# Block one's up projection: a 512-column matmul for the convolved half of pairs 2 to 21, and where the bank rotation starts

## What is computed

```python
h = modulate(rms_norm(x, norm_ffn[l]), sh2, sc2)
x = x + gt2[:, None, :] * conv_gated_ffn(h, ffn_w_up[l], ffn_conv_w[l], ffn_conv_b[l], ffn_w_down[l])
```

## Time and profile before

| | |
|---|---|
| time, median of 3 runs (lowest, highest) | 2118.98 us (2118.73, 2119.17) |
| the profiled execution's own time | 2120.44 us |
| its span | 2118.5 us |
| granted TensorE clock, mean | 1.00 |
| busy: TensorE, weight loads, VectorE, ScalarE, GpSimd | 99%, 90%, 77%, 58%, 1% |

### The profile page before, as it was taken

How to read it: one execution, slowest core, us unless ns; L and a number is a source line. 1 busy time by engine, 2 the same in 40 slices (tenths; PEclk the granted TensorE clock), 3 DMA queues, 4 the chain that set the end, 5 groups by cost and what they waited for, 6 DMA issues and landing times.

```text
span 2118.5 us, 39184 instructions
## 1 busy us (share of the span) xinstructions
PE 2095.2 (99%) x16348; PEld 1902.0 (90%) x16348; DVE 1639.5 (77%) x2519; ACT 1235.6 (58%) x2010; POOL 13.1 (1%) x20
## 2 busy tenths in 40 slices
PE   8999999999999999999999999999999999999999
PEld 7898999999998899998888989888898888998888
DVE  7899789888887788877887656787688765778876
ACT  4754755555755656555655448566475644766554
POOL 0000000000000000000000000000000000000000
PEclk9999999999999999999999999999999999999999
DMA  9566567768644467655555654555555567455553
GB/s 371 198 210 216 175 214 256 243 226 288 224 158 171 163 209 239 204 181 188 188 190 189 230 159 154 203 190 189 189 180 189 189 196 223 140 170 209 189 189 130
DMA packets 122099, 424.57 MB, mean 200 GB/s; under 512 B 13457, under 2 KB 22033, under 8 KB 121154
## 3 DMA queue, kind: packets, MB, share of 16 engines
q1 hardware_dynamic: 121922, 422.06, 59.0%
HBM read 417.68 MB, written 4.33 MB: 199 GB/s over the span
## 4 chain that ended last, share of the span: by engine, by line
PE 90%; ACT 4%; DVE 4%; DMA 1%; issue 1%; POOL 0%; SPq 0%; ACTq 0%; DVEq 0%
PE bank L207 89%; ACT arena L258 2%; DVE arena L213 2%; DMA raw<-W 1%; ACT hi L258 1%; DVE lo L213 1%; PE bank L210 1%; ACT L258 1%; DVE arena L221 0%; DVE ada L230 0%; ACT L250 0%; DVE m L213 0%; DMA xT<-x 0%; ACT ych L258 0%; POOL arena L213 0%
## 5 line engine op out<-in xcount | busy, mean ns | idle before, releaser
L207 PE MATMUL bank<-h,hi 128*128 128x256 f32 (+1 forms) x5248 | 1183.2, 312 | 0.0
L258 ACT ACTIVATE hi<-raw 128x1024 fp32r<-128x1024 f32 x656 | 688.3, 1056 | 537.5 <-PE bank L207 468.4
L207 PE MATMUL bank<-h,lo 128*128 128x256 f32 x3328 | 950.2, 286 | 1.2 <-DVE arena L221 0.7
L207 PEld LDWEIGHTS bank<-h,hi 128*128 128x128 f32 x5248 | 861.4, 190 | 61.1 <-issue 2.6
L213 DVE TENSOR_TENSOR lo<-raw,hi 128x1024 fp32r<-128x1024 f32 x656 | 792.4, 1220 | 99.4 <-ACT hi L258 98.5
L207 PEld LDWEIGHTS bank<-h,lo 128*128 128x128 f32 x3328 | 633.7, 190 | 12.3 <-issue 7.3
L207 PE MATMUL bank<-act,hi 128*128 128x512 f32 x1056 | 370.0, 393 | 0.0
L207 PE MATMUL bank<-act,lo 128*128 128x256 f32 x1056 | 294.7, 279 | 0.0
L207 PEld LDWEIGHTS bank<-act,hi 128*128 128x128 f32 x1056 | 197.9, 187 | 47.3
L207 PEld LDWEIGHTS bank<-act,lo 128*128 128x128 f32 x1056 | 197.9, 187 | 0.0
L258 ACT ACTIVATE arena<-arena 128x256 f32<-128x256 f32 (+4 forms) x202 | 98.6, 493 | 159.6 <-DVE arena L213 151.5
(11 more groups left out here) (152 smaller groups left out, 1942.0 us busy)
## 6 DMA issues: line engine op xcount, KB each, us to landing
raw<-W SPq DMA_DIRECT2D x664, 512.0 KB, 4.0
ada<-WA SPq DMA_DIRECT2D x80, 512.0 KB, 3.7
arena<-WA SPq DMA_DIRECT2D x16, 512.0 KB, 14.2
arena<-conv_rows SPq DMA_DIRECT2D x16, 280.0 KB, 6.4
arena<-taps SPq DMA_DIRECT2D x2, 1792.0 KB, 8.8
p_projected<-arena SPq DMA_DIRECT2D x2, 1024.0 KB, 7.9
arena<-scr SPq DMA_DIRECT2D x16, 128.0 KB, 5.1
arena<-p_projected SPq DMA_DIRECT2D x2, 1024.0 KB, 4.9
```

Of the source, the lines that this page charges most:

```text
L207: return self.done(lambda e: e.matmul(out, l, r, start=start, stop=stop, skip_group_check=True))
L258: return self.done(lambda e: e.activation(out, in_, f, scale=scale, **kw))
```

## The change

`Banks.begin` sets where a pool's turn starts next: at index 0 before each output projection, at index 4 before each down projection. For pairs 2 to 21 `up_in` replaces `pair`: a pair takes two banks, one for the convolved half, in the wide form (256 and 512 columns), one for the gate, in three matmuls of 256 into its first half. ScalarE copies the second half of the convolved bank out (share), VectorE adds the first half to it into the padded buffer (pad), ScalarE makes the first tap with the convolution's weight and bias as scale and bias (tap, for all pairs), and VectorE makes the other two taps. Pairs 0 and 1 keep `first_pairs` and ScalarE's copy.

```diff
--- before.py
+++ after.py
@@ -174,6 +174,9 @@
         before, self.last[pool[n]] = self.last[pool[n]], use
         self.of[use] = pool[n]
         return before
+
+    def begin(self, pool, n):
+        self.turn[pool] = n - 1
 
     def __call__(self, use):
         return self.aps[self.of[use]]
@@ -588,6 +591,7 @@
         thr = [rs_t, var_t]
         pads = [ar[:, 97 * 256 + i * 258:97 * 256 + (i + 1) * 258] for i in range(3)]
         ftmp = [un(101 + i, 1) for i in range(4)]
+        ushare = [un(105 + i, 1) for i in range(2)]
         bias2 = un(45, 16).rearrange("p (h T s) -> p h T s", h=8, T=2)
         hank = un(73, 16).rearrange("p (h T s) -> p h T s", h=8, T=2)
         oneh, relb, vmask, fb = un(97, 2), un(99, 1), un(100, 2), un(102, 2)
@@ -724,6 +728,31 @@
                     pe.mm(t256(banks[n], 0), wl, t256(x, 2 * k), k == 0, False)
                     i = pe.mm(banks[n], wh, t512(x, k), False, k == nk - 1)
                     names = ends + ([use] if k == nk - 1 else [])
+                    if names:
+                        i.then_inc(pe_main, *names)
+                    if ends:
+                        f.tick()
+
+            def up_in(l, ms, turns):
+
+
+                parts = [(m, part) for m in ms for part in ("conv", "gate")]
+                banks = {}
+                for k, n in turns:
+                    m, part = parts[n]
+                    use = ("up", l, m, part)
+                    if k == 0:
+                        banks[n] = take(WIDE, use)
+                    o = banks[n]
+                    wh, wl, ends = tile([("ffn_w_up", l, k, ("c", m * 128 + (FF if part == "gate" else 0)))])
+                    pe.wait_ge(v_main, ("h", ("n2", l), k))
+                    pe.mm(t256(o, 0), wl, t256(hw, 2 * k), k == 0, False)
+                    if part == "conv":
+                        i = pe.mm(o, wh, t512(hw, k), False, k == KD - 1)
+                    else:
+                        pe.mm(t256(o, 0), wh, t256(hw, 2 * k), False, False)
+                        i = pe.mm(t256(o, 0), wh, t256(hw, 2 * k + 1), False, k == KD - 1)
+                    names = ends + ([use] if k == KD - 1 else [])
                     if names:
                         i.then_inc(pe_main, *names)
                     if ends:
@@ -1190,6 +1219,8 @@
                          ys(v_rw, lambda k: ("ys1", l, k // 2), y1h, y1l), 4)
                 elif what == "wout":
                     l, p = q
+                    if p == 0:
+                        ps.begin(WIDE, 0)
                     updates(what, "w_out", l, p, [2 * p, 2 * p + 1], mgw, lambda k: pe.wait_ge(v_main, ("h", ("merged", l), k)),
                             KD, p == 0)
                 elif what == "norm2":
@@ -1210,13 +1241,15 @@
                 elif what == "up":
                     l, m = q
                     if 2 <= m < KF:
-                        pair(WIDE, item, "ffn_w_up", l, [("c", m * 128), ("c", FF + m * 128)], h_in(("n2", l)))
+                        up_in(l, [m], [(k, n) for n in range(2) for k in range(KD)])
                     if m == 12:
                         f.need(l, 5)
                     if l == L - 1 and 12 <= m < 15:
                         flips(ONE, [m - 7])
                 elif what == "down":
                     l, p = q
+                    if p == 0:
+                        ps.begin(WIDE, 4)
                     updates(what, "ffn_w_down", l, p, [2 * p, 2 * p + 1], actw,
                             lambda k: pe.wait_ge(v_main, ("act", ("n2", l), k)), KF)
                 elif what == "f first":
@@ -1899,13 +1932,22 @@
                     l, m = q
                     if 2 <= m < KF:
                         f.tiles(16)
+                    if 2 <= m < KF:
+                        use = ("up", l, m, "conv")
+                        v.wait_ge(a_main, ("share", l, m))
+                        v.wait_ge(g_main, ("pads", l))
+                        if m >= 3:
+                            v.wait_ge(v_main, ("conv", l, m - 3))
+                        v.tt(pads[m % 3][:, 2:258], t256(ps(use), 0), ushare[m % 2], ADD).then_inc(v_main, ("pad", l, m), frees=use)
                     if later is not None:
                         ffn_halves(("n2", l), later, ftmp[later % 4])
                     later = late
                     if late is not None:
+                        use, half = (("up", l, late), 1) if late < 2 else (("up", l, late, "gate"), 0)
                         v.wait_ge(a_main, ("gelu", l, late))
-                        v.tt(ftmp[late % 4], ftmp[late % 4], ps(("up", l, late))[:, 256:512], MUL).then_inc(
-                            v_main, ("product", l, late), frees=("up", l, late))
+                        v.wait_ge(pe_main, use)
+                        v.tt(ftmp[late % 4], ftmp[late % 4], t256(ps(use), half), MUL).then_inc(
+                            v_main, ("product", l, late), frees=use)
                     late = None
                     if m < KF:
                         x, pd = ftmp[m % 4], pads[m % 3]
@@ -1913,10 +1955,7 @@
                         def w(j):
                             return P("ffn_conv_w", l, j * KF + m)
 
-                        v.wait_ge(a_main, ("pad", l, m))
-                        v.wait_ge(g_main, ("pads", l))
-                        v.ts(x, pd[:, 2:258], w(2), P("ffn_conv_b", l, m), MUL, ADD).then_inc(v_main)
-                        v.wait_ge(v_main)
+                        v.wait_ge(a_main, ("tap", l, m))
                         v.stt(x, pd[:, 1:257], w(1), x, MUL, ADD).then_inc(v_main)
                         v.wait_ge(v_main)
                         v.stt(x, pd[:, 0:256], w(0), x, MUL, ADD).then_inc(v_main, ("conv", l, m))
@@ -2516,6 +2555,11 @@
                     l, m = q
                     if 2 <= m < KF:
                         f.tiles(16)
+                    if 2 <= m < KF:
+                        if m >= 4:
+                            a.wait_ge(v_main, ("pad", l, m - 2))
+                        a.wait_ge(pe_main, ("up", l, m, "conv"))
+                        a.act(ushare[m % 2], t256(ps(("up", l, m, "conv")), 1), ACT.Copy).then_inc(a_main, ("share", l, m))
                     if later is not None:
                         ffn_halves(("n2", l), later, ftmp[later % 4], ("product", l, later))
                     later = late
@@ -2524,11 +2568,15 @@
                         a.act(ftmp[late % 4], ftmp[late % 4], ACT.Gelu_apprx_tanh).then_inc(a_main, ("gelu", l, late))
                     late = None
                     if m < KF:
-                        a.wait_ge(pe_main, item)
-                        a.wait_ge(g_main, ("pads", l))
-                        if m >= 3:
-                            a.wait_ge(v_main, ("conv", l, m - 3))
-                        a.act(pads[m % 3][:, 2:258], ps(item)[:, 0:256], ACT.Copy).then_inc(a_main, ("pad", l, m))
+                        if m >= 4:
+                            a.wait_ge(v_main, ("act", ("n2", l), m - 4))
+                        if m < 2:
+                            a.wait_ge(pe_main, item)
+                            a.wait_ge(g_main, ("pads", l))
+                            a.act(pads[m][:, 2:258], ps(item)[:, 0:256], ACT.Copy).then_inc(a_main, ("pad", l, m))
+                        a.wait_ge(a_main if m < 2 else v_main, ("pad", l, m))
+                        a.act(ftmp[m % 4], pads[m % 3][:, 2:258], ACT.Identity, bias=P("ffn_conv_b", l, m),
+                              scale=P("ffn_conv_w", l, 2 * KF + m)).then_inc(a_main, ("tap", l, m))
                         late = m
                     if m == 12:
                         f.need(l, 5)
```

## The result

The changed kernel takes 2124.02 us (median of 9 executions, 2121.95 to 2127.06) against 2119.08 us before: a ratio of 1.0024 [1.0016, 1.0033], 4.9 us slower. The forecast was 2119.2 us, no change, with a range to 2122.2.

What follows compares the result with a forecast made beforehand. TensorE was taken to bound block one's feed-forwards. The wide matmul's -4.26 us, nothing from the other engines and +4.46 us of waits before the down projections made +0.20 us: 2119.2 us, no change, range 2116.8 to 2122.2.

Steps and rivals of the forecast that it cites:

- What bounds the kernel: In block one's feed-forwards, layers 0 and 1, TensorE alone bounds: a microsecond of TensorE is a microsecond of the run.
- So I count no loss of clock for an idle time of 2 us: TensorE's granted clock stays at 2.4 GHz after such idle time, as from 10 to 20 us: no cost added.
- Part 3: Before each layer's down projection TensorE waits for pair 21's pad to release its bank: 2.23 us each, 4.46 us lost.
- Part 1: Up projection's convolved tiles in the wide form save 4.26 us over 320 tiles, or 3.20 us at 0.3500 us each.
- I take 0.3467: Up projection's convolved tile steps at 0.3467 us instead of 0.3600, as block two's does on the same operand h.
- the prediction's own mark of 5.7: Up projection: a pair above 5.7 us would break the wide matmul's gain or the engines' cover; about 5.65 was expected.
- Part 2: Up projection: ScalarE's and VectorE's changed work beside TensorE fits under the weight splits' lead and costs nothing.
- the ring: Up projection, per pair: share, pad, tap, two VectorE taps wait on each other in turn; covered by splits running ahead.
- rival 4: Layer 0's modulation column makes pair 21's pad late: 1.3 us more, 2120.5 us, still no change; chance 0.05.
- The rest of the span shifted but not changed: Outside the changed tiles and the waits before the down projections, the profile only moves in time; no cost added.
- Rival 2: Up projection's wide form saves nothing between gate halves, leaving only the waits before the down projections: 2123.4 us; chance 0.05.
- Rival 1: Banks are already free when TensorE reaches the down projections, so no wait: 2114.7 us, or 2117.0 with one free; chance 0.10.

Runs made afterwards that it cites:

- run 3: Kernel before the change, plus one TensorE wait per layer for pair 21's padded copy ahead of the down projection: 2124.34 us.
- run 2: Changed kernel with the down projection starting at index 0 and the turn set back to 0 behind it: 2120.16 us.
- run 7: run 2 with the gate half in the wide form too, leaving out high weights by low activations: 2114.58 us.
- run 8: run 2 with each 512-column matmul of the up projection cut into two of 256: 2120.16 us.
- run 13: Changed kernel with the down projection's four output pairs at index 2, 0, 4 and 2, and index 0 after them: 2119.14 us.
- run 14: run 13 with 128 empty, already met waits on TensorE's queue at 11 us: 2117.85 us.
- run 5: run 2 with 128 empty, already met waits on TensorE's queue at 11 us: 2118.49 us.
- run 9: Changed kernel with 128 empty, already met waits on TensorE's queue at 11 us: 2124.00 us.
- run 1: The changed kernel measured again, with no edit: 2124.33 us.
- run 6: Kernel before the change with 128 empty, already met waits on TensorE's queue at 11 us: 2121.77 us.
- run 15: Kernel before the change with 256 empty waits on TensorE's queue at 11 us: 2128.76 us.
- run 12: run 10 with the 512-column matmul ahead of the 256-column one in each convolved tile: 2120.73 us.
- run 10: run 2 without setting the turn back to 0 behind the down projection, so the turn runs on: 2120.94 us.
- run 11: run 10 with 128 empty waits on TensorE's queue at 11 us: 2120.82 us.

## Why the prediction was wrong

**What bounds the kernel** was right. Each microsecond that TensorE stood in these stages came out in the total (run 3: two waits of 2.29 us, and 4.4 us more in the executions at 1.000).

**"So I count no loss of clock for an idle time of 2 us" failed**, and it is the largest term missing. It was inferred from one stretch at the start of one execution, which kept its clock over an idle time of 2.93 us (TensorE, before 13.73 us); so did the stop in layer 1 here. But behind such a stop the clock often falls: 1.4 falls per execution of the change at 1.7 us make 2.4 us, by the mean clocks; some of them can belong to other stops (run 2). Part 3 ended at the moment when TensorE starts again, and half of what a stop can cost comes after it.

**Part 1's "I take 0.3467" failed**, in size. The tile takes 0.353 us, outside my ends of 0.3467 and 0.3500: 1.06 and 1.22, together 2.3 us instead of 4.26. A pair takes 114.14 / 20 = 5.71 us, past the prediction's own mark of 5.7. I chose the row with the same operand, but the operand doesn't decide (run 7: 0.353 and 0.347 on h). The rule of the Trainium skill (TensorE: Matmul & The Clock Gate, Back-to-back issue gap) gave 0.8 us in all, also off: the runs have 2.3; the page calls it the gap of an isolated matmul. Either failure alone would have left the sum inside the range (2119.2 + 2.0 = 2121.2, and 2119.2 + 2.4 = 2121.6, against 2122.2); together they take it out.

**Part 2 held.** In layer 0's up projection TensorE is never idle, and the stage has the one table load that it had before (336.07 us, 336.66 before); run 8 puts the ring at nothing in the stage.

```profile
336.00:447.00 111.00, 111.00 (x782) 103.79 (x781) 101.07 (x166) 69.98 (x120) 0.00 (x0) 1.00 0.76 264
```

**Part 3's stop held:** 2 x 2.14 against 4.46. Layer 0's column was not late (rival 4): it ended at 449.44 us and share at 449.54. The Trainium skill's advice on banks (Perfetto Trace Analysis, Optimizing Tensor Performance) agrees with it: the earlier trace rows became a 2.14 us wait when the next group was sent to the bank being emptied.

**"The rest of the span shifted but not changed" failed.** Weight blocks in block two that land just in time come late in part of the executions. Run 13 against 14, run 2 against 5, and the landings in all profiles (last section) show the instruction load among them as a cause. In the profiled execution TensorE lost 0.47 us to it directly. The larger part came after: 304 wide tiles at 0.353 in place of 0.347 us, another 2.0 us. That fits its being the slowest of the nine.

**The sum as it came out:** 2119.1 + 4.3 (stops) - 2.3 (wide form) + 2.4 (clock) = 2123.5, of 2124.0 to 2124.3 measured. The remaining 0.5 to 0.8 us fit the late block near 1360 us, if about one execution in four has it at 2.5 us, which is an estimate. But run 9 did not confirm that, so its share stays open; as do the causes of the late transfers of conv_rows at 1219 us and of a block before 537 us. Rival 2's 2123.4 lies close by chance: the wide form does save. Rival 1, banks free at the seam, had the right cure; measured, it gives 2119.1 (run 13) or 2117.9 (run 14) and not 2114.7.

## What to carry to other kernels

Price a new wait on TensorE with what its clock may do after it: here a stop of 2.1 us cost up to 3.8. A rotation that is one count over the whole program can't be set at one place without looking at the next users of every bank: three settings moved the collision to 450, 1006 and 1327 us before one had none. And where transfers land just in time, a change in the number of instructions can cost or gain time by moving the engine's instruction loads among them: the same 128 empty waits cost 2.9 us in one kernel here and gained 1.7 in another.

## What the runs showed of the hardware

**A wide tile has two steps.** The same pair of matmuls (256 and 512 columns) on h goes at 0.347 or at 0.353 us, and keeps to one for a hundred microseconds. In the changed kernel's profile the step changes at the stop for the late block; the other execution of the same kernel (run 1) had no stop there. 63 tiles of PE's time line, of the first and of the second:

```profile
1372.13 0.39 PE L210 MATMUL bank<-h,hi 128*128 128x512 f32 x1
...
1373.34 0.39 PE L210 MATMUL bank<-h,lo 128*128 128x256 f32 x1 [0.47 <-DVE arena L216]
...
1400.06 0.40 PE L210 MATMUL bank<-h,hi 128*128 128x512 f32 x1
...
1422.32 0.40 PE L210 MATMUL bank<-h,hi 128*128 128x512 f32 x1
```

```profile
1400.03 0.39 PE L210 MATMUL bank<-h,hi 128*128 128x512 f32 x1
...
1421.87 0.39 PE L210 MATMUL bank<-h,hi 128*128 128x512 f32 x1
```

22.26 / 63 = 0.353 and 21.84 / 63 = 0.347. The other profiles agree. TensorE stops inside an up projection of block two in five of the eighteen (the result and runs 2, 6, 13, 15; 0.47 to 0.97 us), and in all five the 304 wide tiles from there to the end of the projection go at 0.353; in the other thirteen the same tiles go at 0.347. Such a stop thus costs twice, 0.5 to 1.0 us at once and 304 x 0.0067 = 2.0 us in the tiles that follow. Not every stop does it: behind the stop at 1006 us, ahead of the first wide tile, the step is 0.347 in runs 2, 5 and 8, while in run 7 some 30 tiles go at 0.353. In layer 1's up projection (run 7) the step went the other way behind pairs 12 to 14, where transposes stand between the tiles. What sets it was not found; the order of the two matmuls doesn't bring 0.347 (run 12: layer 0's 320 tiles take 113.90 us, 334.55 to 448.45, against 114.14).

**A load of instructions delays weight blocks:** one packet of q8 among six blocks, and they land in 6.7 us instead of 5.1 (runs 13, 14). In five of the eighteen profiles (the result and runs 1, 2, 13, 15) such a packet comes 4.6 to 5.8 us after the third block of the burst near 1360 us was issued. That block lands in 8.5 to 9.0 us there, and TensorE stops in four of the five. In ten others no packet comes while it is under way; it lands in 7.3 to 7.5 us, and TensorE doesn't stop there. In runs 10 to 12 the burst is wider apart (the third block comes 2.2 to 2.3 us after the first, not 0.9 to 1.0): 7.2 and 7.4 us with a packet (runs 10, 12), 6.1 us without (run 11), and no stop.
